# Order of the 512- and 256-column products in the feed-forward stages of a two-layer trunk

## The reference, cut to what matters

```python
def conv_glu_ffn(x, w_in, conv_w, conv_b, w_out):
    S = x.shape[1]
    h = x @ w_in                                   # (256, 2048) @ (2048, 2 * 5632)
    hp = jnp.pad(h, ((0, 0), (CONV_WIDTH - 1, 0), (0, 0)))
    hc = conv_b + hp[:, 0:S] * conv_w[0]
    for kk in range(1, CONV_WIDTH):
        hc = hc + hp[:, kk:kk + S] * conv_w[kk]
    gate, val = jnp.split(hc, 2, axis=-1)
    return (jax.nn.gelu(gate, approximate=False) * val) @ w_out
```

## Time and profile before

| | us |
|---|---|
| median of 3 runs | 2067.44 |
| lowest, highest | 2067.41, 2067.52 |
| the profiled execution: its own time | 2068.17 |
| its span, from the first to the last instruction | 2066.1 |
| PE busy in the span | 2048.4 (99%) |
| PE loading weights | 1753.6 (85%) |
| DVE busy | 1443.6 (70%) |
| ACT busy | 884.8 (43%) |
| mean granted clock of PE | 0.998 of full |

### The profile page before, as it was taken

How to read it: one execution, slowest core, us unless ns; L and a number is a source line. 1 busy time by engine, 2 the same in 40 slices (tenths; PEclk the granted TensorE clock), 3 DMA queues, 4 the chain that set the end, 5 groups by cost and what they waited for, 6 DMA issues and landing times.

```text
span 2066.1 us, 27101 instructions
## 1 busy us (share of the span) xinstructions
PE 2048.4 (99%) x10886; PEld 1753.6 (85%) x10886; DVE 1443.6 (70%) x1630; ACT 884.8 (43%) x811; POOL 5.8 (0%) x10
## 2 busy tenths in 40 slices
PE   8999999999999999999999999999999999999997
PEld 7888888888888888888888887888888888888886
DVE  5446566867767677667697886786776768667778
ACT  4443443543443344343434655354344344443441
POOL 0000000000000000000000000000000000000000
PEclk9999999999999999999999999999999999999999
DMA  8654464665555555555556435465555555555552
GB/s 307 205 185 158 146 244 163 232 196 194 191 184 196 188 187 198 184 190 196 184 185 193 140 127 186 163 241 193 194 184 194 191 184 199 186 186 198 184 190 95
DMA packets 194300, 389.54 MB, mean 189 GB/s; under 512 B 6890, under 2 KB 9156, under 8 KB 193220
## 3 DMA queue, kind: packets, MB, share of 16 engines
q1 hardware_dynamic: 193955, 388.49, 56.5%
q10 hardware_dynamic: 288, 0.26, 0.1%
HBM read 386.36 MB, written 2.10 MB: 188 GB/s over the span
## 4 chain that ended last, share of the span: by engine, by line
PE 99%; DVE 1%; DMA 0%; issue 0%; ACT 0%; DVEq 0%
PE ps L1187 36%; PE ps L1197 19%; PE ps L1214 13%; PE ps L1216 12%; PE ps L1215 12%; PE ps L1175 1%; PE ps L1297 1%; PE ps L1565 1%; PE ps L1540 1%; PE ps L1548 1%; PE ps L1264 0%; PE ps L1302 0%; PE ps L1176 0%; PE ps L1414 0%; PE ps L1226 0%; DMA xres<-x 0%
## 5 line engine op out<-in xcount | busy, mean ns | idle before, releaser
L448 ACT ACTIVATE w_hi<-raw 128x2048 fp32r<-128x2048 f32 x355 | 679.3, 1916 | 953.1 <-DMA raw<-ffn_w_in 517.7
L705 DVE TENSOR_TENSOR w_lo<-raw,w_hi 128x2048 fp32r<-128x2048 f32 x355 | 807.8, 2287 | 230.5 <-ACT w_hi L448 229.7
L1187 PE MATMUL ps<-T,w_hi 128*128 128x512 f32 x3264 | 765.0, 390 | 0.0
L1187 PEld LDWEIGHTS ps<-T,w_hi 128*128 128x128 f32 x3264 | 605.8, 188 | 122.9 <-issue 1.7
L1197 PEld LDWEIGHTS ps<-T,w_lo 128*128 128x128 f32 x3264 | 405.8, 192 | 10.0 <-issue 2.0
L1197 PE MATMUL ps<-T,w_lo 128*128 128x256 f32 x3264 | 410.6, 283 | 0.0
L1214 PE MATMUL ps<-w_hi,gT 128*128 128x512 f32 x704 | 274.3, 390 | 0.0
L1216 PE MATMUL ps<-w_hi,gT 128*128 128x512 f32 x704 | 274.1, 389 | 0.0
L1215 PE MATMUL ps<-w_lo,gT 128*128 128x512 f32 x704 | 274.1, 389 | 0.0
L726 DVE TENSOR_TENSOR arena<-ps,half 128x512 f32<-128x512 f32 x96 | 65.5, 688 | 181.7 <-ACT half L503 181.7
L730 DVE SCALAR_TENSOR_TENSOR xres<-ps,xres 128x1024 f32<-128x1024 f32 (+1 forms) x104 | 118.5, 1140 | 87.7 <-PE ps L1216 87.0
(11 more groups left out here) (133 smaller groups left out, 787.8 us busy)
## 6 DMA issues: line engine op xcount, KB each, us to landing
raw<-ffn_w_in SPq DMA_DIRECT2D x176, 1024.0 KB, 5.0
raw<-ffn_w_out SPq DMA_DIRECT2D x88, 1024.0 KB, 5.0
raw<-even_w_in SPq DMA_DIRECT2D x39, 1024.0 KB, 5.2
raw<-attn_w_qkv SPq DMA_DIRECT2D x20, 1024.0 KB, 5.2
raw<-even_w_out SPq DMA_DIRECT2D x16, 1024.0 KB, 5.1
raw<-attn_w_out SPq DMA_DIRECT2D x16, 1024.0 KB, 5.1
arena<-ln_gain SPq DMA_DIRECT2D x4, 1024.0 KB, 6.7
arena<-ln_bias SPq DMA_DIRECT2D x4, 1024.0 KB, 8.8
```

Source lines behind the costliest of these rows:

```text
L448: nc.scalar.activation(w_hi[:, s % RING], raw[:, s % RING], ACT.Copy).then_inc(hi_ready, 1)
L705: vec.tensor_tensor(w_lo[:, s % RING], raw[:, s % RING], w_hi[:, s % RING].bitcast(F32), ALU.subtract).then_inc(lo_ready, 1)
L1187: ins = mm(ps[:, banks[j]], w_hi[:, s % RING, k, P * j:P * j + P], T[:, GK * kg + k], start=kg == 0 and k == 0, stop=kg == KG - 1 and k == ...
```

## The change

`long_products` and `short_products` become functions of their own that take the block, and `hidden` orders a call's products anew. Blocks before ran long 1, short 1, short 2, long 2, long 3, short 3, short 4, long 4. Afterwards: long 1, (the gate's transposes, where asked for), long 2, then short 1, 2, 3, 4, then long 3, long 4. `used` is counted up for block 1 behind short 1, for block 2 behind short 2, for blocks 3 and 4 behind their long products. The waits for the low parts (`ready`) stand ahead of long 1, long 2, short 3 and short 4. `turned_block` keeps its order for the stages outside the feed-forward.

```diff
+            def long_products(s, kg, banks, waits=()):
+
+                for j in range(TPC):
+                    if waits and j % 2 == 0:
+                        pe.wait_ge(*waits[j // 2])
+                    for k in range(GK):
+                        ins = mm(ps[:, banks[j]], w_hi[:, s % RING, k, P * j:P * j + P], T[:, GK * kg + k],
+                                 start=kg == 0 and k == 0, stop=kg == KG - 1 and k == GK - 1)
+                    if s == S_ODD_OUT - 1 and j == 1:
+                        ins.then_inc(queries_half, 1)
+                return ins
+
+            def short_products(s, kg, banks):
+
+                for j in range(TPC):
+                    for k in range(GK):
+                        ins = mm(ps[:, banks[j], 0:SEQ], w_lo[:, s % RING, k, P * j:P * j + P],
+                                 T[:, GK * kg + k, 0:SEQ], start=False, stop=False)
+                return ins
+
             def turned_block(s, kg, banks, waits=()):
 ...
                 if kg % 2 == 0:
-                    long_products()
-                    return short_products()
-                short_products()
-                return long_products()
+                    long_products(s, kg, banks, waits)
+                    return short_products(s, kg, banks)
+                short_products(s, kg, banks)
+                return long_products(s, kg, banks, waits)
 ...
                 def hidden(s, bank, turn=0, waits=(), gate=False):
-                    for kg in range(KG):
+                    banks = range(bank, bank + TPC)
+                    for kg in (0, 1):
                         if kg == 1 and gate:
                             turn_gate()
                         ready(s + kg, turn)
-                        turned_block(s + kg, kg, range(bank, bank + TPC), waits if kg == 0 else ()).then_inc(used, 1)
+                        long_products(s + kg, kg, banks, waits if kg == 0 else ())
+                    for kg in range(KG):
+                        if kg >= 2:
+                            ready(s + kg, turn)
+                        ins = short_products(s + kg, kg, banks)
+                        if kg < 2:
+                            ins.then_inc(used, 1)
+                    for kg in (2, 3):
+                        long_products(s + kg, kg, banks).then_inc(used, 1)
```

More of the change, by code:

```diff
@@ L1177, in turned_mm @@
                           stop=kg == KG - 1 and k == GK - 1)
-            def turned_block(s, kg, banks, waits=()):
[L1181 to L1199, removed]
+            def long_products(s, kg, banks, waits=()):
[8 more added lines that the diff above has]
+                return ins
```

## The result

The changed kernel takes 2070.24 us (median of 22 runs, 2068.83 to 2071.87); the kernel before, in as many runs beside it, 2067.68 us (2067.20 to 2068.44). The ratio is 1.0012, 95% interval 1.0006 to 1.0017: slower by 0.12%, 2.6 us, under the 0.2% taken as the least that can be told for sure, but on the other side of the forecast of 2067.1, and 0.04 us above the range. The spread between these runs is 3.0 us, where the kernel before has 1.2.

The account below looks back on a forecast made before the run. PE's own spacings were taken to bound the kernel; -0.8 us from fewer run-length changes and +0.5 from the two tails gave -0.3, set against the median 2067.44: 2067.1 us, range 2066.2 to 2070.2.

Parts of the forecast that it names:

- What bounds the kernel: Whole kernel: PE waits for nobody except at the start, so the time is the sum of PE's own spacings.
- Part 1: Feed-forward calls: fewer changes of run length gain 0.02 us a call, 0.8 us over 42 calls.
- Rivals B and C: B, slower: short products lose pace in a run of 64, 2076 us, chance 0.04; C, faster by over 0.2%, chance 0.01.
- Part 2: Feed-forward calls: inputs such as blocks' low parts are wanted earlier, by 1.92 or 3.63 us for low parts; cost 0.
- Part 3, ordinary turns: Loop output stages: block 3's slot freed 1.92 us later cuts a 2.89 us lead to 0.97; cost 0 in 18 turns.
- Part 3, tails: Two tails: a lead of 1.70 us against a shift of 1.92; 0.25 us each, 0.5 for both, bounds 0 and 1.
- Part 3, first turns: First loop turn of each feed-forward: lead already 1.0 us, load can land at 415.3; cost 0, bounds 0 and 1.8.
- Two loads 1.92 us apart: cost 0: Loads into the slots of blocks 1 and 2, issued close together, can land later but neither stands before `halves`; cost 0.
- rival A: Load behind block 3 delayed further by crowding; PE waits 1.3 us at output product 4, 18 turns, 23 us, 2090; chance 0.05.

Follow-up runs that it names:

- experiments 9 and 10: ACT copying the halves ahead of rounding the block four further on, repeated on one chip: on the changed kernel 2066.72 us, on the kernel before 2067.89 us.
- experiment 5: The kernel before, products in their old order, with only block 1's slot released late (9.3 us into the call): 2069.26 us.
- the second profile: Profile of the changed kernel run again with no edit: that execution took 2068.29 us, the median of its runs was 2069.78 us.

## Why the prediction was wrong

- **What bounds the kernel**, PE's own spacings, was right, and so was what follows from it: the change acts by pace and by new waits.
- **Part 1** was right: 22.21 us a call, 120 ns a short product in the run of 64, the gain 0.8 to 0.95 us, which experiments 9 and 10 bear out. Rivals B and C did not come. The figures of the Trainium skill, "TensorE: Matmul & The Clock Gate", section "Back-to-back issue gap", one for 512 and one for 256 columns, by which the order is worth nothing, miss the 0.02 us; the measurement decides.
- **Part 2** was right: no row shows PE waiting for low parts in the feed-forward.
- **Part 3, ordinary turns**: right in mechanism and size. ACT's copies 1.9 us later, a lead of 1.0 us left, no wait in any of the 16 turns that are not the first.
- **Part 3, tails**: right in mechanism, small in size: 0.25 us each taken, 0.44 and 0.49 measured; the upper bound of 0.5 held them. The 0.2 us of missing lead was right; what was too small is the 0.3 us that the addition has to be ahead.
- **Part 3, first turns**: this is the step that failed. I took 0 with an upper bound of 1.8 for both; 2.15 + 0.99 came in the first profile, 0.73 + 0 in the second, and the median of the 22 runs asks for 2.6 + 0.8 - 0.9 = 2.5. The taken value assumed that the queue ahead of the critical load drains by the time of its later issue, so that it lands 5.0 us after it. It did not: with 8.1 and 7.0 us from issue to landing in the first profile and 6.7 and 5.9 in the second, ACT rounds it 0.6 to 2.9 us later after the output's start than before. Block 1's late release moves one load more than 3 us back, right ahead of the last output block and the parameters, and this alone costs 1.72 us (experiment 5). The bound failed by two things. It assumed that the load moves by no more than its own issue, 1.92 us; in the first profile the chain moved by 2.9, and PE then waited twice, at product 3 as well as at product 4. And it let PE wait only when the whole lead of 1.0 us is gone, where the stage loses from 0.7 on; by that estimate 1.92 would have cost 1.2 us a turn, 2.4 for both.
- **"Two loads 1.92 us apart: cost 0"** failed for the same reason. I asked only whether the bunched loads themselves stand ahead of `halves`, not what queue behind them does. In experiment 5 the critical load takes 8.8 us from issue to rounding where a lone load takes 479.97 - 474.71 = 5.3. The page that I set beside rival A (the Trainium skill, "DMA: Bandwidth & Descriptors", section "Issuing engines are not separate DMA queues") has transfers share the engines and interleave. The trace agrees that loads in flight together slow each other; that they interleave it does not show: in the first profile `ln_gain` and `ln_bias`, issued at 402.72 and 403.27, take 8.7 and 10.6 us and so land at 411.4 and 413.9, 2.5 us apart and in the order of their issue.
- **Rival A** was this mechanism, at the same product and with DVE's addition as what PE waits for, but I put it in all 18 turns for 23 us and, in the forecast's own sum, left it out of the two turns in which the lead was already 1.0 us.

The sign follows: -0.8 + 0.9 alone would have been no change; the first turns made it 2.6 us. The interval of the first comparison, 1.0006 to 1.0017, is clear of 1; those of the single experiments are 0.0009 wide to each side, 1.9 us, and most of them touch 1, so the account rests on the stages in the traces, which agree to some hundredths of a us.

## What to carry to other kernels

When a slot is freed later, add up what else is in the transfer queue at that moment: a load that nobody waits for can push the one behind it that somebody does. Look for the turn in which the lead is already smallest, here the first, where other loads are mixed in, and bound the delay there by the whole queue and not by the shift of one issue. And a short copy on which PE depends should not stand in its engine's order behind a conversion that waits for a transfer: moving it ahead made the change harmless here, and its small gain visible.

## What was unexpected

The page's DMA issues show how far a crowded queue reaches: a parameter load of 1 MB took 6.7 and 8.8 us (median to landing, gain and bias) in the kernel before, and in the kernel after:

```profile
arena<-ln_gain SPq DMA_DIRECT2D x4, 1024.0 KB, 7.4
arena<-ln_bias SPq DMA_DIRECT2D x4, 1024.0 KB, 9.5
```

though SP issues them where it did, right behind the last output block's load. One load moved by more than 3 us slowed the two behind it by 0.7 us, as a median over all four pairs of which only two lie in a first turn. The critical one behind those took 8.2 us between issue and rounding in the first profile's first turn, against 7.3 before, but 6.8 in the second profile's. The other thing is the spread of the runs: 1.2 us in the kernel before, 3.0 in the changed one, and 0.6 and 0.9 with the halves first, where no wait of PE hangs on a landing. That the landings make the spread is argued and not shown: the kernel before, with no such wait, spreads over 2.0 and 1.8 us in the later sets of 33 runs, and a part lies ahead of the feed-forward, whose first output stage starts between 412.93 and 413.93 in the traces.
